# Hyena spectra: sums formed by VectorE from the accumulators, a smaller ScalarE copy, another order in the first unit, a buffer of its own for the last low products

## The chip, the cores and the metric

The program runs on one core of one Trainium2 chip. The metric is the device time of one execution in microseconds, median of several runs; lower is better. Engines are named as in the profile: PE (TensorE, matmuls), DVE (VectorE), ACT (ScalarE), POOL (GpSimd), SP (SyncE, which here only starts transfers).

## What is computed

Two transformer blocks on a sequence of 512 tokens of width 1024. The change touches only the Hyena mixer of the second block, whose core is a long convolution done through spectra, for two orders `o`:

```python
k2 = jnp.concatenate([fwd, jnp.zeros_like(fwd[:1]), bwd[1:][::-1]], axis=0)
k2 = k2 / jnp.sum(jnp.abs(k2), axis=0, keepdims=True)
kf = jnp.fft.rfft(k2, axis=0)
gates = (x1, x2)
zc = v
for o in range(HY_ORDER):
    zf = jnp.fft.rfft(zc.astype(jnp.float32), n=2 * L, axis=1)
    y = jnp.fft.irfft(zf * kf[None, :, o], n=2 * L, axis=1)[:, :L]
    zc = gates[o] * (y.astype(h.dtype) + skip[o] * zc)
return zc @ w_out
```

`fwd` and `bwd` are filters: the output of a small network, times a decay. L is 512.

## The kernel before

The whole program is one hand-ordered stream for each engine. Engines meet at semaphores alone: `then_inc(y_kc, 1)` raises one when an instruction ends, `wait_ge(y_kc, n)` holds the queue of an engine until it stands at n. Each queue runs strictly in order, so what is written first goes first.

The spectral stage works in four **units** u = 0 to 3: two orders times two halves of the 1024 channels. A unit's signal and filter are transformed with cosine and sine tables (`t_fwd`), in two halves f of the frequencies of 128 rows each, and back with `t_inv`. Since the spectrum of a real signal can be folded, the even and the odd time samples are transformed apart, and sums and differences of the two give the low and the high frequencies.

The steps of one unit, with their names in the code:

- `filter_tile(u, t, b)` (PE, L1684): two matmuls of the filter network's last layer into the accumulator banks b and b+1 of `ps`; `filter_out` (DVE, L2859, L2860) multiplies them with the decay DEC into PM, `y_pm`; `filter_abs` (ACT, L2228) writes their absolute values to the one buffer AB, `y_ab`, and waits for the sum before it, `y_n`; `filter_sum` (DVE, L2868 to L2872) adds them up in AS, `y_n`; `filter_norm` (PE) and `norm_out` (DVE) make the divisor.
- `turn_in(u)` (PE, L1728): transposes of the signal U into banks 4 and 5; `turned_in` (ACT, L2247) copies them to ZK, `y_tc`.
- `k_transform(u, f)` (PE, L1743): the filter's spectrum into banks 0 to 3 (cosine even, cosine odd, sine even, sine odd). `k_out` (ACT, L2253) copies all four to KS, `y_kc`. `k_parts` (POOL, L1129 to L1132) forms two sums and two differences of them in KP, `y_kp`. The next k_transform, and filter tiles that use these banks, wait for `y_kc`.
- `z_transform(u, f)` (PE, L1758): the signal's spectrum into banks 4 to 7; `z_even` (ACT, L2259) copies banks 4 and 6 to XZ.
- `multiply(u, f)` (DVE): the parts of z (L2899 to L2903, from XZ and banks 5 and 7, `y_x`), then the complex products in two halves (L2911 to L2917), each of six operations, into YB, `y_cb`.
- `y_parts(u, f)` (POOL, L1140 to L1144): sums and differences of YB into YF, `y_y`. For u > 0 it waits until `inverse(u - 1)` has read YF (`y_inv`).
- `inverse(u)` (PE, L1780): back to time; `gated` (DVE, L2934, L2936) scales, adds the skip term (`skipped`, ACT, L2267), and multiplies with the gate into U, `y_z`, from which the unit two later starts.

The four units overlap by hand: while DVE multiplies unit u, PE transforms the filter of u + 1 and the signal of u + 1, and the filter tiles of u + 2. In unit 0 the filter of unit 1 is also made inside this stage, in two pairs of tiles in banks 0 to 3, one pair ahead of z_transform(0,1) and one behind. In the last unit, the output projection (L536 to L538) follows directly on the last products.

KS has four rows of 512, and lies behind YF and ZK.

Of the kernel before, what the change touches and what calls it, by code (L numbers as in the profile page):

```python
# [122 lines left out]
def build(nc, A, out, stop=None):  # L123

    ctx = ExitStack()
    with ctx:
# [902 lines left out]
        def _(pool):  # L1029
# [93 lines left out]
            def k_parts(u, f):  # L1123

                pool.wait_ge(y_kc, 2 * u + f + 1)
                if u:
                    pool.wait_ge(y_cb, 4 * (u - 1) + 2 * f + 2)
                ce, co, se, so = (KS[:, n, :] for n in range(4))
                pool.tensor_tensor(KP[:, f, 0, :], ce, co, ALU.add)  # L1129
                pool.tensor_tensor(KP[:, f, 1, :], se, so, ALU.add)  # L1130
                pool.tensor_tensor(KP[:, f, 2, :], ce, co, ALU.subtract)
                pool.tensor_tensor(KP[:, f, 3, :], so, se, ALU.subtract).then_inc(y_kp, 1)  # L1132
# [1872 lines left out]
```

## Time and profile before

| | us |
|---|---|
| median of 3 runs | 2882.75 |
| lowest, highest | 2882.46, 2883.8 |
| the profiled execution: its time | 2882.58 |
| the profiled execution: its span | 2880.8 |
| PE busy in the span | 2777.3 (96%) |
| DVE, ACT, POOL busy | 1303.6 (45%), 712.7 (25%), 1606.7 (56%) |

The span is one execution from first to last instruction as the profiler recorded it; its time has a little around it. Busy time is the time in which an engine has an instruction in work. In the timelines below each row has a start in us from the span's start, a duration in us, the engine, the line of the code, the tiles written and read, and in brackets how long the engine idled before it and who released it. A row of PE with x16 is a merged run of 16 records; a float32 matmul leaves two. The granted clock (PEclk) of PE is 1.00 at 2.4 GHz and 0.50 at 1.2 GHz.

### The profile page before, as it was taken

The page shows a single profiled execution, that of the slowest core. Times are in us where ns is not written, and L with a number is a line of the kernel's source. Part 1 is how long each engine was busy: PE and PEld are TensorE (multiplying, and loading weights), DVE is VectorE, ACT ScalarE, POOL GpSimd, SP SyncE. Part 2 cuts the span into 40 slices and gives each one's busy share as a digit, 9 for nine tenths or more (in the row PEclk, how much of TensorE's full clock was granted, in tenths as well). Part 3 has the DMA queues.
Part 4 walks back from the last instruction along what each step waited for, and adds up shares of the span by engine and source line. Part 5 has one row for each costly group of instructions (what it writes and reads, how often), then busy time and mean ns, then how long its engine had stood idle before and what let it go on. Part 6 is the DMA issues. An engine that isn't in the chain of part 4 may idle for free.

```text
span 2880.8 us, 39841 instructions
## 1 busy us (share of the span) xinstructions
PE 2777.3 (96%) x15611; PEld 2250.4 (78%) x15611; DVE 1303.6 (45%) x1924; ACT 712.7 (25%) x1102; POOL 1606.7 (56%) x1569
## 2 busy tenths in 40 slices
PE   7999989999999999999999999999999898999999
PEld 7998888799678878888865568888777454788887
DVE  6787562211710564333346633331286678433311
ACT  3375224432620111110036621110111222211100
POOL 7652124655077766666641157766675534676764
PEclk9999999999999999999999999999999999999999
DMA  4221001222022564555530013332322100233331
GB/s 131 84 64 36 2 2 55 78 82 81 1 85 92 194 214 161 188 192 190 183 102 16 30 59 102 90 106 101 104 88 92 37 1 15 88 102 89 108 101 69
DMA packets 292585, 260.22 MB, mean 90 GB/s; under 512 B 6617, under 2 KB 264390, under 8 KB 292156
## 3 DMA queue, kind: packets, MB, share of 16 engines
q1 hardware_dynamic: 289492, 250.83, 27.1%
q0 software_dynamic: 2416, 6.34, 0.7%
q8 instruction: 117, 1.92, 0.3%
q10 hardware_dynamic: 504, 0.66, 0.1%
q14 instruction: 56, 0.46, 0.0%
HBM read 255.72 MB, written 2.10 MB: 89 GB/s over the span
## 4 chain that ended last, share of the span: by engine, by line
PE 87%; DVE 6%; issue 4%; DVEq 2%; ACT 2%; DMA 0%; POOL 0%; POOLq 0%; SPq 0%; ACTq 0%
PE ps L536 24%; PE ps L537 23%; PE ps L538 23%; PE ps L1780 2%; PE ps L1621 1%; PE ps L1758 1%; PE ps L1601 1%; PE ps L1611 1%; PE ps L1743 1%; PE ps L1366 1%; PE ps L1345 1%; PE ps L947 1%; DVE YB L2913 1%; PE ps L1373 1%; DVEq L2915 1%
## 5 line engine op out<-in xcount | busy, mean ns | idle before, releaser
L825 POOL CAST spl<-raw 128x512 fp32r<-128x512 f32 (+1 forms) x352 | 247.7, 704 | 635.0 <-PE ps L538 503.6
L536 PE MATMUL ps<-HSH,spl 128*128 128x512 f32 x1344 | 535.9, 399 | 20.4 <-DVE HSL L747 16.2
L827 POOL TENSOR_TENSOR spl<-raw,spl 128x512 fp32r<-128x512 f32 (+1 forms) x352 | 497.0, 1412 | 56.3 <-issue 6.5
L537 PE MATMUL ps<-HSL,spl 128*128 128x512 f32 x1344 | 527.3, 392 | 0.0
L538 PE MATMUL ps<-HSH,spl 128*128 128x512 f32 x1344 | 527.0, 392 | 0.0
L831 POOL TENSOR_TENSOR spl<-raw,spl 128x512 fp32r<-128x512 f32 (+1 forms) x352 | 481.2, 1367 | 51.5 <-issue 1.5
L536 PE MATMUL ps<-HNH,spl 128*128 128x264 f32 (+1 forms) x1152 | 364.7, 317 | 4.0 <-DVE HNL L717 3.6
L537 PE MATMUL ps<-HNL,spl 128*128 128x264 f32 (+1 forms) x1152 | 356.0, 309 | 0.0
L538 PE MATMUL ps<-HNH,spl 128*128 128x264 f32 (+1 forms) x1152 | 355.0, 308 | 0.0
L829 POOL CAST spl<-raw 128x512 fp32r<-128x512 f32 (+1 forms) x352 | 232.1, 659 | 206.8 <-PE ps L538 204.9
L536 PEld LDWEIGHTS ps<-HSH,spl 128*128 128x128 f32 x1344 | 254.2, 189 | 95.7 <-issue 38.5
L538 PEld LDWEIGHTS ps<-HSH,spl 128*128 128x128 f32 x1344 | 254.7, 190 | 54.3
L537 PEld LDWEIGHTS ps<-HSL,spl 128*128 128x128 f32 x1344 | 255.0, 190 | 52.6 <-issue 2.2
L536 PEld LDWEIGHTS ps<-HNH,spl 128*128 128x128 f32 x1152 | 217.5, 189 | 19.3 <-issue 5.2
L537 PEld LDWEIGHTS ps<-HNL,spl 128*128 128x128 f32 x1152 | 217.6, 189 | 13.3 <-issue 1.9
L538 PEld LDWEIGHTS ps<-HNH,spl 128*128 128x128 f32 x1152 | 216.9, 188 | 10.9
L536 PE MATMUL ps<-AFH,spl 128*128 128x512 f32 x528 | 206.2, 391 | 0.0
L538 PE MATMUL ps<-AFH,spl 128*128 128x512 f32 x528 | 205.6, 389 | 0.0
L537 PE MATMUL ps<-AFL,spl 128*128 128x512 f32 x528 | 205.5, 389 | 0.0
L2698 DVE TENSOR_TENSOR ps<-SG,ps 128x512 f32<-128x512 f32 x66 | 45.9, 696 | 259.7 <-PE ps L538 255.6
L2687 DVE SCALAR_TENSOR_TENSOR H<-ps,pcol,H 128x512 f32<-128x512 f32 x32 | 24.0, 751 | 276.5 <-PE ps L538 276.5
L937 DVE SCALAR_TENSOR_TENSOR ps<-adw,csil,ps 128x512 f32<-128x512 f32 x144 | 108.7, 755 | 46.5 <-DMA adw<-in_ada_w 36.0
(459 smaller groups left out, 4386.6 us busy)
## 6 DMA issues: line engine op xcount, KB each, us to landing
adw<-in_ada_w SPq DMA_DIRECT2D x96, 512.0 KB, 5.6
raw<-in_w_in SPq DMA_DIRECT2D x44, 1024.0 KB, 5.0
raw<-in_ffn_w_up SPq DMA_DIRECT2D x88, 512.0 KB, 4.6
raw<-in_w_ffn_in SPq DMA_DIRECT2D x44, 512.0 KB, 4.7
raw<-in_ffn_w_down SPq DMA_DIRECT2D x16, 1408.0 KB, 5.9
raw<-in_hy_w_in SPq DMA_DIRECT2D x12, 1024.0 KB, 5.0
raw<-in_w_ffn_out SPq DMA_DIRECT2D x8, 1408.0 KB, 6.4
raw<-in_w_branch_dn SPq DMA_DIRECT2D x8, 1024.0 KB, 4.9
```

The lines of the kernel that those rows point to most:

```text
L536: pe.matmul(dst, w[0], x[0], start=first, stop=False)
L537: pe.matmul(dst, w[0], x[1], start=False, stop=False)
L538: return pe.matmul(dst, w[1], x[0], start=False, stop=final)
L825: pool.tensor_copy(hi[:, first, :], w[:, first, :])
L827: pool.tensor_tensor(lo[:, first, :], w[:, first, :], hi[:, first, :], ALU.subtract).then_inc(split_first, 1)
L829: pool.tensor_copy(hi[:, second, :], w[:, second, :])
L831: pool.tensor_tensor(lo[:, second, :], w[:, second, :], hi[:, second, :], ALU.subtract).then_inc(split_ready, 1)
L937: ins = dve.scalar_tensor_tensor(ads[:, j % 2, :] if k == KD - 1 else acc, w, scale, acc, ALU.mult, ALU.add)
L947: mm = pe.matmul(ps[:, 4, ds(n, 1)], ads[:, j % 2, m * P:(m + 1) * P], ones[:, 0:1], start=True, stop=True)
L1345: mm = pe.matmul(ps[q, b, h * HALF:(h + 1) * HALF], G["lmp"][l % 2][q, h, :], G["yp"][q, h, :] if l else ident[q, q], start=True, stop=True)
L1780: mm = pe.matmul(dst, YF[:, f, e * 2 + s, c * P:(c + 1) * P], t_inv[:, s, f, e * SEQ // 2:(e + 1) * SEQ // 2], start=f + s == 0, stop=f + ...
L2698: dve.tensor_tensor(prod, SG[:, r % 2, :], ps[:, 2 * b, :], ALU.mult).then_inc(acc_free[b], 1)
```

## The change

- **k_parts moves from POOL to DVE.** ACT copies only banks 0 and 2 (the even parts) to KS, now of two rows; DVE adds and subtracts them with banks 1 and 3 read in place. Since banks 1 and 3 are now free only when DVE is done, PE's waits for `y_kc` become waits for `y_kp`, which DVE raises.
- **Unit 0 has another order.** z_transform(0,1) goes ahead of all filter tiles of unit 1; the four tiles follow in a row in banks 0, 2, 4 and 6. DVE does the parts of z of (0,1), the four filter products, and then the products of multiply(0,1) and the filter sums. turn_in(1) goes ahead of k_transform(1,1).
- **YL**, a buffer of four rows where KS was (and where KS now has two), takes the low products of the last unit, y_parts(3,0), which no longer waits for inverse(2).

```diff
@@
-        KS = fresh("KS", 4, SEQ)
+        ks_at = here[0]
+        KS = fresh("KS", 2, SEQ)
+        YL = at("YL", [4, SEQ], ks_at)
@@
+        def y_of(u, f, n):
+            return YL[:, n, :] if (u, f) == (UNITS - 1, 0) else YF[:, f, n, :]
@@ pool
             def y_parts(u, f):
-                if u:
+                if u and (u, f) != (UNITS - 1, 0):
                     pool.wait_ge(y_inv, u * NT)
...
-                if u + 1 < UNITS:
-                    k_parts(u + 1, 0)
                 y_parts(u, 1)
-                if u + 1 < UNITS:
-                    k_parts(u + 1, 1)
@@ tensor
             def k_transform(u, f):
                 if f:
-                    pe.wait_ge(y_kc, 2 * u + 1)
+                    pe.wait_ge(y_kp, 2 * u + 1)
...
             def filters(u):
                 filter_tile(u, 0, LATE_BANK[0])
-                pe.wait_ge(y_kc, 2 * u)
+                pe.wait_ge(y_kp, 2 * u)
...
             k_transform(0, 1)
-            pe.wait_ge(y_kc, 2)
-            filter_tile(1, 0, 0)
-            filter_tile(1, 1, 2)
             z_transform(0, 1)
-            pe.wait_ge(y_pm, NT + 1)
-            filter_tile(1, 2, 0)
-            pe.wait_ge(y_pm, NT + 2)
-            filter_tile(1, 3, 2)
+            pe.wait_ge(y_kp, 2)
+            for t in range(NT):
+                if t == 2:
+                    pe.wait_ge(y_x, 2)
+                filter_tile(1, t, FIRST_BANK[t])
@@ scalar
-                act.activation(KS[:, :, :], ps[:, 0:4, :], ACT.Copy).then_inc(y_kc, 1)
+                act.activation(KS[:, :, :], ps[:, 0:4:2, :], ACT.Copy).then_inc(y_kc, 1)
@@ vector
+            def k_parts(u, f):
+                dve.wait_ge(y_kc, 2 * u + f + 1)
+                dve.tensor_tensor(KP[:, f, 0, :], KS[:, 0, :], ps[:, 1, :], ALU.add)
+                dve.tensor_tensor(KP[:, f, 1, :], KS[:, 1, :], ps[:, 3, :], ALU.add)
+                dve.tensor_tensor(KP[:, f, 2, :], KS[:, 0, :], ps[:, 1, :], ALU.subtract)
+                dve.tensor_tensor(KP[:, f, 3, :], ps[:, 3, :], KS[:, 1, :], ALU.subtract).then_inc(y_kp, 1)
...
+            k_parts(0, 0)
             multiply(0, 0)
-            filter_out(1, 0, 0)
-            filter_out(1, 1, 2)
+            k_parts(0, 1)
+            parts_of_z(0, 1)
+            for t in range(NT):
+                filter_out(1, t, FIRST_BANK[t])
+            multiply(0, 1, parts=False)
             filter_sum(1, 0)
             filter_sum(1, 1)
-            filter_out(1, 2, 0)
-            filter_out(1, 3, 2)
-            multiply(0, 1)
+            k_parts(1, 0)
             filter_sum(1, 2)
             filter_sum(1, 3)
+            k_parts(1, 1)
...
             multiply(1, 0)
+            k_parts(2, 0)
             multiply(1, 1)
+            k_parts(2, 1)
...
             multiply(2, 0)
+            k_parts(3, 0)
             multiply(2, 1)
+            k_parts(3, 1)
             multiply(3, 0)
```

The first place is ACT in unit 0, from the transposes of unit 0 (ZK) to the skip terms of unit 0 (ytmp). Before:

```order
L2247 ACTIVATE ZK<-ps 128x512 [waits y_t] x4
L2253 ACTIVATE KS<-ps 128x2048 [waits y_k]
L2259 ACTIVATE XZ<-ps 128x1024 [waits y_dft]
L2253 ACTIVATE KS<-ps 128x2048 [waits y_kp,y_k]
L2228 ACTIVATE AB<-PM 128x1024 [waits y_n,y_pm] x2
L2259 ACTIVATE XZ<-ps 128x1024 [waits y_cb,y_dft]
L2228 ACTIVATE AB<-PM 128x1024 [waits y_n,y_pm]
L2253 ACTIVATE KS<-ps 128x2048 [waits y_kp,y_k]
L2228 ACTIVATE AB<-PM 128x1024 [waits y_n,y_pm]
L2247 ACTIVATE ZK<-ps 128x512 [waits y_t] x4
L2253 ACTIVATE KS<-ps 128x2048 [waits y_kp,y_k]
L2267 ACTIVATE ytmp<-U,pcol 128x512 [waits y_conv] x2
```

The same place with the change:

```order
L2238 ACTIVATE ZK<-ps 128x512 [waits y_t] x4
L2244 ACTIVATE KS<-ps 128x1024 [waits y_k]
L2250 ACTIVATE XZ<-ps 128x1024 [waits y_dft]
L2244 ACTIVATE KS<-ps 128x1024 [waits y_kp,y_k]
L2250 ACTIVATE XZ<-ps 128x1024 [waits y_cb,y_dft]
L2219 ACTIVATE AB<-PM 128x1024 [waits y_n,y_pm] x2
L2244 ACTIVATE KS<-ps 128x1024 [waits y_kp,y_k]
L2238 ACTIVATE ZK<-ps 128x512 [waits y_t] x4
L2219 ACTIVATE AB<-PM 128x1024 [waits y_n,y_pm] x2
L2244 ACTIVATE KS<-ps 128x1024 [waits y_kp,y_k]
L2258 ACTIVATE ytmp<-U,pcol 128x512 [waits y_conv] x2
```

The two AB copies of filter tiles (1,0) and (1,1) now stand behind the XZ copy of (0,1), and both ahead of the KS copy of k_transform(1,0) and the ZK copies of unit 1.

The second place is PE in unit 1, from the last transposes of turn_in(2) through the filter tiles of unit 3 to inverse(1); W_157 and A_158 are the weights and activations of the filter network. Before:

```order
L1728 MATMUL ps<-square,U 128x128 [waits y_tc]
L1728 MATMUL ps<-square,U 128x128 x3
L1684 MATMUL ps<-W_157,A_158 128x512 [waits y_w,y_am]
L1684 MATMUL ps<-W_157,A_158 128x512
L1684 MATMUL ps<-W_157,A_158 128x512 [waits y_kc]
L1684 MATMUL ps<-W_157,A_158 128x512 x3
L1684 MATMUL ps<-W_157,A_158 128x512 [waits y_tc]
L1684 MATMUL ps<-W_157,A_158 128x512
L1780 MATMUL ps<-t_inv,YF 128x256 [waits y_pm,y_y]
```

With the change:

```order
L1718 MATMUL ps<-square,U 128x128 [waits y_tc]
L1718 MATMUL ps<-square,U 128x128 x3
L1674 MATMUL ps<-W_157,A_158 128x512 [waits y_w,y_am]
L1674 MATMUL ps<-W_157,A_158 128x512
L1674 MATMUL ps<-W_157,A_158 128x512 [waits y_kp]
L1674 MATMUL ps<-W_157,A_158 128x512 x3
L1674 MATMUL ps<-W_157,A_158 128x512 [waits y_tc]
L1674 MATMUL ps<-W_157,A_158 128x512
L1770 MATMUL ps<-t_inv,YF 128x256 [waits y_pm,y_y]
```

The order is the same; the second tile's wait for ACT's copy has become a wait for DVE's sums.

The third place is DVE at the end of multiply(1,1). Before:

```order
L2916 TENSOR_TENSOR YB<-YB,YT 128x512
L2917 TENSOR_TENSOR YB<-YB,YT 128x512
L2859 TENSOR_TENSOR PM<-ps,DEC 128x512 [waits y_f,y_ab,y_w]
L2860 TENSOR_TENSOR PM<-ps,DEC 128x512
L2859 TENSOR_TENSOR PM<-ps,DEC 128x512 [waits y_f]
```

With the change:

```order
L2920 TENSOR_TENSOR YB<-YB,YT 128x512
L2921 TENSOR_TENSOR YB<-YB,YT 128x512
L2892 TENSOR_TENSOR KP<-KS,ps 128x512 [waits y_kc]
L2893 TENSOR_TENSOR KP<-KS,ps 128x512
L2894 TENSOR_TENSOR KP<-KS,ps 128x512
L2895 TENSOR_TENSOR KP<-ps,KS 128x512
L2853 TENSOR_TENSOR PM<-ps,DEC 128x512 [waits y_f,y_ab,y_w]
```

k_parts(2,1), four operations, stands between the last product and the filter products of unit 3.

## Rows read from the trace of the kernel before

**Rows 1.** The page of the profile: its head, and the chain's shares by engine.
```profile
span 2880.8 us, 39841 instructions
...
PE 87%; DVE 6%; issue 4%; DVEq 2%; ACT 2%; DMA 0%; POOL 0%; POOLq 0%; SPq 0%; ACTq 0%
```

**Rows 2.** Timeline of PE, 2225 to 2470: start, us, engine, line, [idle before <-releaser].
```profile
2260.13 3.60 PE L1684 MATMUL ps<-W,A 128*128 128x512 f32 x8
...
2266.13 8.76 PE L1743 MATMUL ps<-PM,t_fwd 128*128 128x512 f32 x16 [2.41 <-DVE PM L2860]
...
2276.85 7.13 PE L1743 MATMUL ps<-PM,t_fwd 128*128 128x512 f32 x16 [1.97 <-ACT KS L2253]
...
2294.99 13.98 PE L1780 MATMUL ps<-t_inv,YF 128*128 128x256 f32 x64
...
2350.51 15.74 PE L1780 MATMUL ps<-t_inv,YF 128*128 128x256 f32 x64 [2.91 <-DVE PM L2860]
...
2407.58 7.17 PE L1780 MATMUL ps<-t_inv,YF 128*128 128x256 f32 x32 [2.76 <-POOL YF L1144]
...
2433.67 6.90 PE L1780 MATMUL ps<-t_inv,YF 128*128 128x256 f32 x24 [5.15 <-POOL YF L1144]
...
2445.54 11.25 PE L1780 MATMUL ps<-t_inv,YF 128*128 128x256 f32 x40 [4.97 <-DVE U L2936]
...
2456.44 0.58 PE L536 MATMUL ps<-ZH,spl 128*128 128x512 f32 x1
```

**Rows 3.** Timeline of DVE, same columns, 2225 to 2447.
```profile
2242.04 0.69 DVE L2899 TENSOR_TENSOR XZ<-XZ,ps 128x512 f32<-128x512 f32 x1 [14.44 <-ACT XZ L2259]
...
2257.52 0.68 DVE L2860 TENSOR_TENSOR PM<-ps,DEC 128x512 f32<-128x512 f32 x1
...
2331.88 0.69 DVE L2899 TENSOR_TENSOR XZ<-XZ,ps 128x512 f32<-128x512 f32 x1 [1.22 <-ACT XZ L2259]
...
2334.69 1.55 DVE L2911 TENSOR_TENSOR YB<-XZ,KP 128x512 f32<-128x512 f32 x1 [0.16 <-issue]
...
2341.67 0.69 DVE L2911 TENSOR_TENSOR YB<-XZ,KP 128x512 f32<-128x512 f32 x1
...
2433.63 0.69 DVE L2911 TENSOR_TENSOR YB<-XZ,KP 128x512 f32<-128x512 f32 x1 [7.98 <-POOL YF L1144]
...
2437.59 0.69 DVE L2911 TENSOR_TENSOR YB<-XZ,KP 128x512 f32<-128x512 f32 x1
...
2443.76 0.75 DVE L2934 SCALAR_TENSOR_TENSOR ytmp<-ps,rn,ytmp 128x512 f32<-128x512 f32 x1 [0.16 <-issue]
```

**Rows 4.** Groups by line, 2225 to 2460: busy us, mean ns | idle before, releaser.
```profile
L2913 DVE TENSOR_TENSOR YB<-XZ,KP 128x512 f32<-128x512 f32 x16 | 20.6, 1284 | 0.0
...
L2899 DVE TENSOR_TENSOR XZ<-XZ,ps 128x512 f32<-128x512 f32 x8 | 5.5, 688 | 27.2 <-ACT XZ L2259 27.1
...
L2253 ACT ACTIVATE KS<-ps 128x2048 f32<-128x2048 f32 x8 | 15.0, 1876 | 32.8 <-PE ps L1743 32.8
...
L2259 ACT ACTIVATE XZ<-ps 128x1024 f32<-128x1024 f32 x8 | 8.2, 1021 | 49.7 <-PE ps L1758 33.6 <-DVE YB L2917 16.2
...
L2228 ACT ACTIVATE AB<-PM 128x1024 f32<-128x1024 f32 x12 | 12.7, 1056 | 26.8 <-DVE PM L2860 16.4 <-DVE AS L2872 8.7 <-DVE AS L2868 1.7
...
L1129 POOL TENSOR_TENSOR KP<-KS 128x512 f32<-128x512 f32 x8 | 10.9, 1359 | 36.4 <-ACT KS L2253 36.4
```

**Rows 5.** Timeline of POOL, 2215 to 2470.
```profile
2256.14 1.72 POOL L1140 TENSOR_TENSOR YF<-YB 128x512 f32<-128x512 f32 x1
...
2428.61 1.26 POOL L1140 TENSOR_TENSOR YF<-YB 128x512 f32<-128x512 f32 x1 [15.28 <-PE ps L1780]
```

**Rows 6.** Busy time of stretches: length, each engine's busy us, PEclk, DMA share, GB/s.
```profile
2266.00:2269.50 3.50, 3.37 (x4) 1.51 (x5) 3.17 (x6) 0.00 (x0) 1.83 (x3) 0.51 0.42 95
...
2408.00:2411.50 3.50, 3.50 (x18) 3.09 (x17) 3.34 (x4) 0.00 (x0) 3.50 (x3) 1.00 0.00 0
...
2446.00:2449.50 3.50, 3.50 (x9) 2.56 (x9) 3.42 (x5) 2.01 (x4) 2.61 (x3) 0.50 0.02 5
```

More of the change, by code:

```diff
@@ L1121, in filter_in @@
                 pool.dma_start(DEC[:, :, :], dec[:, :, half_d]).then_inc(y_w, 16)
-            def k_parts(u, f):
-                pool.wait_ge(y_kc, 2 * u + f + 1)
-                if u:
[L1127 to L1132, printed above, removed]
             def y_parts(u, f):
-                if u:
+                if u and (u, f) != (UNITS - 1, 0):
                     pool.wait_ge(y_inv, u * NT)
                 c, si, cm, sm = (YB[:, n, :] for n in range(4))
+                y = [y_of(u, f, n) for n in range(4)]
                 pool.wait_ge(y_cb, 4 * u + 2 * f + 1)
-                pool.tensor_tensor(YF[:, f, 0, :], c, cm, ALU.add)
-                pool.tensor_tensor(YF[:, f, 2, :], c, cm, ALU.subtract)
+                pool.tensor_tensor(y[0], c, cm, ALU.add)
+                pool.tensor_tensor(y[2], c, cm, ALU.subtract)
                 pool.wait_ge(y_cb, 4 * u + 2 * f + 2)
-                pool.tensor_tensor(YF[:, f, 1, :], si, sm, ALU.subtract)
-                pool.tensor_tensor(YF[:, f, 3, :], si, sm, ALU.add).then_inc(y_y, 1)
+                pool.tensor_tensor(y[1], si, sm, ALU.subtract)
+                pool.tensor_tensor(y[3], si, sm, ALU.add).then_inc(y_y, 1)
             pool_split(pool, hy_in, behind_second=mlp_in)
@@ L1789, in inverse @@
                 else:
-                    pe.wait_ge(y_kc, 2 * UNITS)
+                    pe.wait_ge(y_kp, 2 * UNITS)
                 for c in cs:
@@ L1795, in inverse @@
                         for f in range(2):
-                            mm = y_products(ps[:, c % 2 if u + 2 < UNITS else c, e * SEQ // 2:(e + 1) * SEQ // 2], c, e, f)
+                            mm = y_products(u, ps[:, c % 2 if u + 2 < UNITS else c, e * SEQ // 2:(e + 1) * SEQ // 2], c, e, f)
                     mm.then_inc(y_inv, 1)
@@ L1821, in _ @@
                     z_transform(u, 1)
+                else:
+                    turn_in(u + 1)
                 k_transform(u + 1, 1)
-                turn_in(u + 1)
+                if u:
+                    turn_in(u + 1)
                 if u + 2 < UNITS:
@@ L2277, in _ @@
             k_out(0, 1)
+            z_even(0, 1)
             filter_abs(1, 0)
-            filter_abs(1, 1)
-            z_even(0, 1)
-            filter_abs(1, 2)
             for u in range(UNITS):
@@ L2284, in _ @@
                     z_even(u, 0)
+                if u == 0:
+                    filter_abs(1, 1)
                 if u + 1 < UNITS:
                     k_out(u + 1, 0)
+                if 0 < u < UNITS - 1:
+                    z_even(u, 1)
                 if u == 0:
+                    turned_in(1)
+                    filter_abs(1, 2)
                     filter_abs(1, 3)
+                    k_out(1, 1)
                 elif u + 1 < UNITS:
-                    z_even(u, 1)
-                if u + 1 < UNITS:
                     turned_in(u + 1)
@@ L2894, in _, with parts_of_z @@
                         norm_out(0, 6)
-            def multiply(u, f):
+            def k_parts(u, f):
[4 more added lines that the diff above has]
+                dve.tensor_tensor(KP[:, f, 3, :], ps[:, 3, :], KS[:, 1, :], ALU.subtract).then_inc(y_kp, 1)
+            def parts_of_z(u, f):
                 dve.wait_ge(y_zc, 2 * u + f + 1)
@@ L2903, in multiply @@
                 dve.tensor_tensor(XZ[:, 1, :], XZ[:, 1, :], ps[:, 7, :], ALU.add).then_inc(y_x, 1)
+            def multiply(u, f, parts=True):
+                if parts:
+                    parts_of_z(u, f)
                 dve.drain()
-                dve.wait_ge(y_kp, 2 * u + f + 1)
                 if u or f:
```

15 lines of the change are left out of this document (7 added, 8 removed).

## The prediction

> **What bounds the kernel now.** The page of the profile comes first: of a span of 2880.8 us, PE carries 87% of the chain that ended last and DVE 6% [rows 1]. The diff touches one stage only, the spectral part of the Hyena mixer, from the last projection tile to the first matmul of the output projection at 2456.44. So the timelines of that stage are read next, and in them PE's brackets: how long PE idled and for whom. Rows 2 hold the places. PE waits 2.41 us for the filter product PM ahead of k_transform(1,0), 1.97 us for the copy KS, 2.91 us for PM ahead of inverse(1), 2.76 us for YF ahead of inverse(2), and 5.15 and 4.97 us in the last unit [rows 2]. Between these waits PE's work is the same before and after; the change moves only the waits. Behind every one of them stands a chain on DVE, so DVE's timeline [rows 3] gives the prices, and the groups by line [rows 4] the means.
>
> **Prices.** A multiply() is three pieces on DVE. The even and odd parts of z take 2.74 us in unit 0 (2242.04 to the first product, 0.69 us an operation) and 2.81 us at 2331.88 [rows 3]. A half of the products takes 3.96 us where POOL is quiet (2433.63 to 2437.59) and 6.17 us where POOL forms YF beside it (2437.59 to 2443.76); where POOL still forms KP, as at 2334.69 to 2341.67, it takes 6.98 us [rows 3]. The reason is visible in one operation: L2913, with both inputs in SBUF, has a mean of 1284 ns, against 688 ns for L2899, which has one input in ps [rows 4]. L2860 with an input in ps took 0.68 us at 2257.52 [rows 3], while POOL's L1140 was running from 2256.14 [rows 5]. So I cost the new k_parts on DVE, four operations of L2899's form, at about 0.61 us start to start, 2.5 us in all with the semaphore wait, and do not stretch it beside POOL. Its bounds are 2.4 us (four at the pace of rows 3) and 4.7 us (two of the four held up by POOL as a half of products is, (6.17 - 3.96) / 2 = 1.1 us each).
> The Trainium skill speaks against this price (VectorE: DVE Perf Modes, section "The TRN2 errata"): its table gives VectorE 120 fixed cycles from PSUM and 58 from SBUF at 0.96 GHz. Here the two are 688 ns and 0.69 us, so the trace does not agree; by the page five k_parts on the path would add about 5 x 4 x 65 ns = 1.3 us, an estimate.
> On ACT, KS shrinks from four banks, 1876 ns, to two, which I take at the 1021 ns of XZ, an activation of 1024 elements [rows 4]. POOL loses eight times four operations with a mean near 1359 ns [rows 4]; this is worth time only where POOL was late or in DVE's way. A pair of filter tiles takes 3.60 us, so 1.72 us a tile, start to start; a transform takes 7.1 us for 16 records [rows 2].
>
> **Unit 0: a loss.** Until 2242.04 nothing moves: k_parts(0,0) ends near 2237.7, hidden behind z_transform(0,0). multiply(0,0) then takes 2.7 + 4.0 + 6.2 us and ends near 2254.9, k_parts(0,1) near 2257.4, and PE, which has finished z_transform(0,1) at 2254.5, waits 3.0 us for it. Four tiles and the last filter_out follow; k_transform(1,0) starts near 2266.0, where it starts now (2266.13 [rows 2]). But DVE now has the products of multiply(0,1) behind the filter products, 4.0 + 6.2 us, to 2276.1. Only then comes filter_sum(1,0), and this matters, since the new ACT order puts filter_abs(1,1) ahead of k_out(1,0): the single buffer AB must be read first. Queued on ACT behind it are KS and all four ZK copies. So: first sum 0.7 us (2276.8), AB 1.06 us (2277.9), KS 1.0 us (2278.9); meanwhile filter_sum(1,1) to 2280.4; k_parts(1,0) 2.5 us, and k_transform(1,1) starts at 2282.9 instead of 2276.85, 6.1 us later. Behind it, 18.1 us now pass until inverse(0) at 2294.99 [rows 2]; then it will be 6.9 for the transform, 1.2 for the copy, 2.6 for k_parts, 0.9 for the norm and 5.2 for three tiles, 16.8 us, since the turn_in lies in the hole: -1.3 us. The clock: k_transform(1,0) took 8.76 us where the later one took 7.13 [rows 2], with a granted clock of 0.51 in its first 3.5 us [rows 6], so a restart after such a wait costs 1.7 us. It is now hidden for k_transform(1,0) and comes back at k_transform(1,1), ahead of which PE idles 5.4 and 2.5 us with 1 us of transposes between: +1.7. Unit 0 gives **+6.5 us**.
>
> **Unit 1: a loss.** multiply(1,0) is unchanged. k_parts(2,0), 2.5 us, takes the place of DVE's 1.22 us wait for XZ [rows 3], which it covers: +1.3. The first half of multiply(1,1) no longer has POOL beside it: 6.98 - 3.96 = -3.0. DVE is then 1.7 us earlier. But k_parts(2,1), 2.5 us, follows, and filter tile (3,1) now waits for it (y_kp) where it waited for ACT's copy (y_kc), done long before. Three tiles, 5.2 us, which now hide behind DVE, stand in the open: -1.7 + 2.5 + 5.2, and 0.1 for the signal, is 6.1 us against the 2.7 us by which inverse(1) now follows the last product. **+3.4 us**. The wait of 2.91 us and its clock loss [rows 2] move from inverse(1) to the tiles.
>
> **Unit 2: even.** The same trade (+1.3, -3.0, +2.5) brings k_parts(3,1) to the moment at which YF is ready. k_transform(3,1) waits 3.0 us for k_parts(3,0), and z_transform(3,0) ends just where the 2.76 us wait [rows 2] ends now. **+0.1 us**.
>
> **Unit 3: the gain.** z_transform(3,0) ends later, so DVE starts multiply(3,0) 2.85 us later; its first half loses POOL's company, -3.0; its second half gains it, +2.2, since y_parts(3,0) writes YL and no longer waits for inverse(2) (POOL waited 15.28 us for it [rows 5]); the two gated() take 0.9 us more beside POOL. Together +2.9. In return DVE's wait of 7.98 us for YF [rows 3] goes. The products of multiply(3,1), and with them the 4.97 us wait of PE and the output projection, come 8.0 - 2.9 = 5.1 us earlier against inverse(2). What is late next is the same DVE chain, now without a hole. **-5.1 us**.
>
> **Sum.** 6.5 + 3.4 + 0.1 - 5.1 = +4.9 us, with three clock losses as now. Two restarts are new, both after 3.0 us of idle: the tiles behind k_parts(0,1), and k_transform(3,1). Of the five waits over 2.3 us in rows 2, four are followed by slow records; the one of 2.76 us is not (7.17 us for 32, granted clock 1.00 [rows 6]). Two times 1.7 us at four in five is +2.7. Total **+7.6 us**. The profiled run took 2882.58 us with its span of 2880.8, 0.2 us under the median of 2882.75, so the forecast is 2882.58 + 7.6 = **2890.2 us**.
>
> **Rivals.**
> - *The clock forgives* (the other side, not slower). If neither new restart falls to 0.5, the sum is +4.9, 2887.5; if the hole in unit 0 costs nothing either, about +3, 2885.5. A measurement of this kernel can tell about 0.2%, 5.8 us, so this is no change. It decides at the two waits of 3.0 us: with one of them charged the sum is 6.6. For it speaks the 2.76 us wait, against it the 2.41 us one, which was charged. 0.32.
> - *The clock takes more.* PE's two short bursts of work between long waits at the end now had 0.50 still 4 us after the restart [rows 6] and lost 2.5 us (11.25 for 40 records). If the hole of unit 0 does that, and both restarts are charged: +10 to +12, 2893 to 2895. I count it with the forecast: 0.60 for both.
> - *POOL and k_parts collide.* Then five k_parts grow by up to 2.2 us: up to +11 on the forecast, 2896 to 2901. Rows 3 and 5 show the form untouched. 0.03.
> - *Faster.* This needs DVE's order in unit 0 not to bite: were filter_sum(1,0) done before 2270, unit 0 would lose nothing and the total would be -1 to +1, still no change; over 5.8 us faster also needs all restarts free and a second gain of 5 us. The wait of filter_abs(1,1) on the sum is in the code. 0.05, with all else I have not seen.
>
> **Numbers.** Slower by over 0.2%: 0.60 + 0.03 = 0.63; within 0.2%: 0.32; faster: 0.05. The range takes in both clock cases: 2884.0 to 2895.5.
>
> **What would show it.** PE idle for DVE's k_parts near 2254 to 2257; an ACT wait of some 14 us at the second AB behind a DVE sum; k_transform(1,1) at 2283; tile (3,1) released by k_parts(2,1); no wait of DVE for YL or YF in unit 3; the granted clock at 0.5 in the four restarts. If k_parts takes more than 2.7 us, if half a multiply beside nothing is not 4.0 us, or if k_transform(1,1) starts before 2278, the prediction is wrong in that step.

## The result, and the profile after

| | before | changed |
|---|---|---|
| median of 13 runs, us | 2882.75 (2881.11 to 2886.26) | 2890.75 (2887.72 to 2893.5) |
| profiled run, us; its span, us | 2882.58; 2880.8 | 2890.96; 2889.2 |
| mean granted clock in the profiled run | 0.985 | 0.982 |

The ratio is 1.0024, with a 95% interval from 1.0017 to 1.0031: the changed kernel is slower by 8.0 us, where 7.6 had been forecast. The head of the page and the chain by engine answer to [rows 1]:

```profile
span 2889.2 us, 39827 instructions
...
PE 2782.8 (96%) x15611; PEld 2252.9 (78%) x15611; DVE 1316.7 (46%) x1956; ACT 706.6 (24%) x1102; POOL 1564.2 (54%) x1537
...
PE 87%; DVE 6%; issue 4%; DVEq 2%; ACT 1%; DMA 0%; POOL 0%; POOLq 0%; SPq 0%; ACTq 0%
```

POOL has lost 42.5 us of work (it had 1606.7) and DVE has gained 13.1 (it had 1303.6), and the chain is the same, PE and then DVE. The totals say nothing of where the 8 us are. The timeline of PE does; it answers to [rows 2], with the same columns:

```profile
2225.90 1.11 PE L1718 MATMUL ps<-square,U 128*128 128x128 f32 x8
...
2258.80 7.14 PE L1674 MATMUL ps<-W,A 128*128 128x512 f32 x16 [2.80 <-DVE KP L2895]
2267.32 7.13 PE L1733 MATMUL ps<-PM,t_fwd 128*128 128x512 f32 x16 [1.38 <-DVE PM L2854]
2274.30 1.11 PE L1718 MATMUL ps<-square,U 128*128 128x128 f32 x8
2281.86 1.98 PE L1718 MATMUL ps<-square,U 128*128 128x128 f32 x8 [6.45 <-ACT ZK L2238]
2284.90 8.60 PE L1733 MATMUL ps<-PM,t_fwd 128*128 128x512 f32 x16 [1.05 <-DVE KP L2895]
...
2297.13 1.05 PE L1681 MATMUL ps<-ones,AS 128*128 128x1 f32 x8 [1.91 <-DVE KP L2895]
2298.04 7.09 PE L1674 MATMUL ps<-W,A 128*128 128x512 f32 x12
2304.97 13.98 PE L1770 MATMUL ps<-t_inv,YF 128*128 128x256 f32 x64
...
2343.21 10.16 PE L1733 MATMUL ps<-PM,t_fwd 128*128 128x512 f32 x16 [2.76 <-DVE KP L2895]
...
2359.87 6.94 PE L1674 MATMUL ps<-W,A 128*128 128x512 f32 x12 [2.40 <-DVE KP L2895]
2366.65 13.98 PE L1770 MATMUL ps<-t_inv,YF 128*128 128x256 f32 x64
...
2404.88 7.13 PE L1733 MATMUL ps<-PM,t_fwd 128*128 128x512 f32 x16 [2.76 <-DVE KP L2895]
...
2422.06 7.07 PE L1770 MATMUL ps<-t_inv,YF 128*128 128x256 f32 x32
...
2454.45 3.78 PE L1770 MATMUL ps<-t_inv,YL 128*128 128x256 f32 x8 [6.36 <-DVE U L2940]
2458.02 7.34 PE L1770 MATMUL ps<-t_inv,YF 128*128 128x256 f32 x32
2465.01 0.58 PE L539 MATMUL ps<-ZH,spl 128*128 128x512 f32 x1
```

The start of each inverse() cuts the stage into four pieces, unit 0 from turn_in(0) to inverse(0), and so on; unit 3 ends with the first matmul of the output projection. The table gives their lengths in us, for both kernels and for six others of the next section, each from its own timeline of PE. The last column but one is the time that PE's records lost to the clock. It is worked out from the records: sixteen of 128x512 take 7.03 us at the full clock, twelve 5.4, eight 3.6, sixty-four of 128x256 13.98, forty 8.8, thirty-two 7.07, twenty-four 5.34, eight about 1.8, and what a row takes beyond that is counted. Not counted are excesses of about 0.1 us and the transposes of 128x128 (0.9 us behind the long wait for ZK in e2 and in the changed kernel, where PE waits again behind them). The column is good to some 0.1 us, and it is the sum over all rows, on the critical path or off it.

| kernel | unit 0 | unit 1 | unit 2 | unit 3 | stage | clock loss | ratio to before (95%) |
|---|---|---|---|---|---|---|---|
| before | 70.48 | 55.52 | 57.07 | 48.86 | 231.93 | 7.5 | |
| before, second profile (e11) | 71.22 | 55.50 | 57.08 | 49.04 | 232.84 | 9.7 | |
| changed | 79.07 | 61.68 | 55.41 | 42.95 | 239.11 | 10.2 | 1.0024 (1.0017 to 1.0031) |
| YL alone (e1) | 70.49 | 55.52 | 57.08 | 42.86 | 225.95 | 5.2 | 0.9979 (0.9970 to 0.9988) |
| YL and the new order, sums on POOL (e2) | 72.04 | 55.52 | 58.37 | 43.12 | 229.05 | 6.7 | 0.9986 (0.9977 to 0.9995) |
| e2 with the first sum ahead (e7) | 67.69 | 55.50 | 57.07 | 44.18 | 224.44 | 6.7 | 0.9976 (0.9966 to 0.9987) |
| YL and sums on DVE, old order (e3) | 89.29 | 60.58 | 57.11 | 42.73 | 249.71 | 12.7 | 1.0061 (1.0047 to 1.0075) |
| changed, with the first sum ahead (e4) | 75.08 | 58.88 | 55.41 | 42.91 | 232.28 | 7.4 | 1.0000 (0.9991 to 1.0009) |
| e1 with PE kept busy at two waits (e8) | 71.52 | 56.48 | 55.31 | 42.76 | 226.07 | 3.4 | 0.9977 (0.9968 to 0.9986) |

The ratios go by runs of the kernel before that were made beside each kernel, with medians of 2882.5 to 2884.0 us, so they differ by up to 0.0006 from quotients with 2882.75.

Between the kernel before and the changed one, units 0 and 1 lose 8.6 and 6.2 us, and units 2 and 3 gain 1.7 and 5.9: +7.2 us in all. The profiled runs differ by 8.4. The other 1.2 us lie outside the stage, which starts at 2225.90 where it started at 2224.51 (1.4 us later, of which 0.2 come back behind it). That is no work of the change: the two profiles of one and the same kernel before start it at 2224.51 and 2225.27, and in the twelve profiles of this study it starts anywhere between 2222.58 and 2226.73. So the stage's length is the better measure, and it is used below.

Four rows explain most of the changed kernel. They stand in the timelines of ACT, of DVE, and of DVE again, in units 0, 1 and 3:

```profile
2279.35 1.06 ACT L2219 ACTIVATE AB<-PM 128x1024 f32<-128x1024 f32 x1 [15.57 <-DVE AS L2862]
```
```profile
2277.53 1.73 DVE L2862 TENSOR_TENSOR AS<-AB 128x512 f32<-128x512 f32 x1 [0.16 <-issue]
...
2357.34 0.69 DVE L2892 TENSOR_TENSOR KP<-KS,ps 128x512 f32<-128x512 f32 x1 [1.39 <-ACT KS L2244]
...
2442.54 0.69 DVE L2915 TENSOR_TENSOR YB<-XZ,KP 128x512 f32<-128x512 f32 x1
```

ACT stands 15.57 us at the second AB copy, because the sum that frees AB runs at 2277.53 on DVE, behind the products of multiply(0,1). k_parts(2,1) finds KS late by 1.39 us. And the first product of multiply(3,1), which waited 7.98 us for YF in [rows 3], waits for nothing.

### The profile page after: what moved, and what is told of

Read it like the earlier page. It is cut to its first block, busy times and chain, and to the rows that moved or that the text cites. A ratio compares the mean times of both kernels' runs of the same rounds, so it can differ in the third digit from the quotient of the medians.

```text
span 2889.2 us, 39827 instructions
## 1 busy us (share of the span) xinstructions
PE 2782.8 (96%) x15611; PEld 2252.9 (78%) x15611; DVE 1316.7 (46%) x1956; ACT 706.6 (24%) x1102; POOL 1564.2 (54%) x1537
## 4 chain that ended last, share of the span: by engine, by line
PE 87%; DVE 6%; issue 4%; DVEq 2%; ACT 1%; DMA 0%; POOL 0%; POOLq 0%; SPq 0%; ACTq 0%
PE ps L539 24%; PE ps L540 23%; PE ps L541 23%; PE ps L1770 1%; PE ps L1733 1%; PE ps L1611 1%; PE ps L1748 1%; PE ps L1674 1%; PE ps L1591 1%; PE ps L1601 1%; PE ps L1356 1%; PE ps L1335 1%; PE ps L953 1%; PE ps L1363 1%; PE ps L1267 1%
```

## The experiments

**Each half of the change alone.** Four kernels take the change apart: YL, the order of unit 0, and the place of the sums. e1 is the kernel before with only this:

```diff
+        ks_at = here[0]
         KS = fresh("KS", 4, SEQ)
+        YL = at("YL", [4, SEQ], ks_at)
...
-                if u:
+                if u and (u, f) != (UNITS - 1, 0):
                     pool.wait_ge(y_inv, u * NT)
+                if (u, f) == (UNITS - 1, 0):
+                    pool.wait_ge(y_kp, 2 * UNITS)
```

> Kernel before plus one part of the change alone: the low products of the last unit go to a buffer of their own (YL, laid over KS, which has been read by then), so y_parts(3,0) no longer waits for inverse(2). KP stays on POOL, the orders stay. Theory (the step on unit 3 of the prediction, and the gain of 5.9 us seen there in the changed kernel): DVE's wait of 7.98 us for YF goes, the products of multiply(3,1) and the output projection come 4.8 to 5.9 us earlier; 2877 to 2878 us, against 2882.75. Rival: the gain of the last stretch belongs to POOL freed from KP, and with KP still there y_parts(3,0) comes no earlier than multiply(3,1) needs it, or the ten final us lose it again in a deeper clock loss: under 2 us gained, 2881 to 2883 us.

Measured: 2877.14 us, ratio 0.9979, 6 us faster; all of it lies in unit 3, 42.86 us against 48.86. Two timelines of e1, of POOL and of PE:

```profile
2414.08 1.76 POOL L1148 TENSOR_TENSOR YL<-YB 128x512 f32<-128x512 f32 x1 [2.66 <-DVE YB L2925]
```
```profile
2438.44 3.54 PE L1788 MATMUL ps<-t_inv,YL 128*128 128x256 f32 x8 [6.57 <-DVE U L2944]
2441.82 7.07 PE L1788 MATMUL ps<-t_inv,YF 128*128 128x256 f32 x32
2448.53 0.58 PE L538 MATMUL ps<-ZH,spl 128*128 128x512 f32 x1
```

POOL's first operation on YL follows DVE's YB after 2.66 us, not inverse(2), for which the same operation waited 15.28 us in [rows 5]. The theory holds, and the rival falls: the gain needs no freed POOL.

e2 is the changed kernel with k_parts back on POOL and a KS of four banks, and with the order of unit 0 and YL as changed:

```diff
-        KS = fresh("KS", 2, SEQ)
+        KS = fresh("KS", 4, SEQ)
...
+            k_parts(0, 0)
+            k_parts(0, 1)
             y_parts(0, 0)
...
-                act.activation(KS[:, :, :], ps[:, 0:4:2, :], ACT.Copy).then_inc(y_kc, 1)
+                act.activation(KS[:, :, :], ps[:, 0:4, :], ACT.Copy).then_inc(y_kc, 1)
...
-            k_parts(0, 0)
             multiply(0, 0)
-            k_parts(0, 1)
```

> The changed kernel with one part undone: the four sums KP are again formed on POOL from a four-bank copy on ACT; the new order of unit 0 and YL stay. Theory (the sums on DVE are what costs): order and YL together stand 3.2 us under the kernel before, by adding up the durations of the rows, and the new place of the sums costs 7 to 10 us; 2879 to 2881 us. Rival (the new order of unit 0 is what costs, since the products of multiply(0,1) stand ahead of filter_sum(1,0)): the loss of 6 to 8.6 us in unit 0 stays and only units 1 and 2 recover 4 us; 2886 to 2888 us.

Measured: 2880.38 us, ratio 0.9986. The stage takes 229.05 us, 2.9 under before (3.2 had been worked out) and 10.1 under the changed kernel. So the sums on DVE cost 10 us in the new order, up to 3.5 of them by a larger clock loss, and without them the new order costs 1.6 us in unit 0. The rival, the order as the whole cause, falls: it left 6 to 8.6 us in unit 0. But the sum that frees AB is late here too, as ACT's timeline of e2 shows, and e4 and e7 below price that:

```profile
2274.78 1.06 ACT L2237 ACTIVATE AB<-PM 128x1024 f32<-128x1024 f32 x1 [11.73 <-DVE AS L2880]
```

e3 is the other half undone, the order of unit 0 as before on PE, ACT and DVE, with the sums on DVE:

```diff
-            z_transform(0, 1)
             pe.wait_ge(y_kp, 2)
-            for t in range(NT):
-                if t == 2:
-                    pe.wait_ge(y_x, 2)
-                filter_tile(1, t, FIRST_BANK[t])
+            filter_tile(1, 0, 0)
+            filter_tile(1, 1, 2)
+            z_transform(0, 1)
+            pe.wait_ge(y_pm, NT + 1)
+            filter_tile(1, 2, 0)
+            pe.wait_ge(y_pm, NT + 2)
+            filter_tile(1, 3, 2)
```

> The changed kernel with the other part undone: unit 0 runs in the order of the kernel before on PE, ACT and DVE; the sums stay on DVE and YL stays. Theory (the sums cost, the order repays part of it): with two filter sums, two filter copies and then both k_parts ahead of it on DVE the first product of multiply(0,1) comes later still; adding up the rows puts the output projection 12 us behind the kernel before with the old order and YL, 8 us behind the changed kernel; 2895 to 2899 us. Rival (the order is what costs): the 8.6 us that the changed kernel loses in unit 0 come back but for the 2.5 us of one k_parts on the path; 2884 to 2886 us.

Measured: 2901.06 us, ratio 1.0061; the stage takes 249.71 us, 10.6 more than in the changed kernel. The theory had 8, and its 2895 to 2899 us were missed by 2; the clock column accounts for the rest, 12.7 us lost here against 10.2. The rival, 2884 to 2886 us, falls by 15 us. Its timeline of PE shows why the order was changed at all:

```profile
2255.83 6.33 PE L1674 MATMUL ps<-W,A 128*128 128x512 f32 x8 [9.66 <-DVE KP L2891]
...
2289.62 9.94 PE L1733 MATMUL ps<-PM,t_fwd 128*128 128x512 f32 x16 [8.64 <-DVE KP L2891]
```

PE's first filter tile needs banks that only k_parts(0,1) frees, and k_parts(0,1) is queued on DVE behind all of multiply(0,0): 9.66 us of waiting, and 8.64 us at the next such place. The four kernels make a square. The new order costs 3.1 us of stage with the sums on POOL (229.05 - 225.95) and saves 10.6 with the sums on DVE (249.71 - 239.11). The sums on DVE cost 23.8 us in the old order and 10.1 in the new. Neither edit has a price of its own. These four differences hold the clock with the work: by the clock column up to 1.5, 2.5, 7.5 and 3.5 us of them, in the order named.

**The queue on DVE in unit 0.** e4 is the changed kernel with one filter sum ahead of the products, and k_parts(1,0) ahead of the second:

```diff
+            filter_sum(1, 0)
             multiply(0, 1, parts=False)
-            filter_sum(1, 0)
-            filter_sum(1, 1)
             k_parts(1, 0)
+            filter_sum(1, 1)
             filter_sum(1, 2)
```

> The changed kernel with DVE's order changed in two places of unit 0: filter_sum(1,0) stands ahead of the products of multiply(0,1), and k_parts(1,0) ahead of filter_sum(1,1). Theory (unit 0 loses because AB, and behind it KS and ZK on ACT, wait for a sum that is queued behind ten us of products): ACT's wait of 15.6 us at the second AB shrinks to about 5, k_transform(1,1) is released some 4 us earlier, the products end 0.7 us later; 3.7 us under the changed kernel, 2887.0 us, within 1.5. Rival (PE in unit 0 is held by the products and the clock, not by the sum): within 1 us of the changed kernel, 2890 to 2892 us.

Measured: 2883.77 us, ratio 1.0000, 7 us under the changed kernel, where 3.7 were expected. The timelines of ACT and PE:

```profile
2266.37 1.06 ACT L2219 ACTIVATE AB<-PM 128x1024 f32<-128x1024 f32 x1 [4.18 <-DVE AS L2862]
```
```profile
2279.07 8.83 PE L1733 MATMUL ps<-PM,t_fwd 128*128 128x512 f32 x16 [3.36 <-DVE KP L2895]
```

ACT waits 4.18 us instead of 15.57, and k_transform(1,1) starts 54.77 us after the start of the stage instead of 59.00: unit 0 is 4.0 us shorter, as the theory has it. The other 2.8 us are in unit 1, where nothing was changed: k_transform(2,1) loses 1.7 us to the clock instead of 3.1, and the tiles behind it, which lost 1.5, lose nothing.

e7 makes the same edit with the sums on POOL:

```diff
+            filter_sum(1, 0)
             multiply(0, 1, parts=False)
-            filter_sum(1, 0)
             filter_sum(1, 1)
```

> The sums on POOL, YL, the new order of unit 0, and filter_sum(1,0) ahead of the products of multiply(0,1): everything of the change but the sums on DVE, with the order mended. Theory: unit 0 took 72.0 us with the sums on POOL and the new order; its k_transform(1,1) waited for ACT's copies, which waited for the sum; the sum ahead takes 2 to 3 us off, so unit 0 takes 69 to 70 us, about one less than the order of before, and the whole stage 224.5 to 227: 2876 to 2878 us, level with the kernel that has YL alone. Rival (with KP on POOL, k_transform(1,1) and the products are bound by KP, not by the sum): unit 0 stays at 72 us, 2880 us.

Measured: 2876.08 us, ratio 0.9976. Unit 0 takes 67.69 us, 4.35 less than in e2 and 2.8 less than before; 2 to 3 had been expected. Part of the 4.35 is clock: k_transform(1,1) lost 1.7 us in e2, and nothing here, where PE waits 1.51 us for ZK instead of 4.16. It is the fastest kernel of the study by its median, but its interval and that of YL alone overlap nearly whole, so that the reordering has gained nothing that the times can tell. In the stage it is 1.5 us ahead of YL alone, after a clock loss that is 1.5 us larger.

**The price of one k_parts.** e6b is the changed kernel with the four sums of k_parts(2,1) formed twice, and a drain between:

```diff
             def k_parts(u, f, again=False):
                 dve.wait_ge(y_kc, 2 * u + f + 1)
+                if again:
+                    dve.tensor_tensor(KP[:, f, 0, :], KS[:, 0, :], ps[:, 1, :], ALU.add)
...
+                    dve.drain()
```

> The changed kernel with the four sums of k_parts(2,1) formed twice on DVE (the same values, a drain of DVE between the two sets). It measures the price of one k_parts and whether that of (2,1) lies on the path to inverse(1), as the step on unit 1 of the prediction has it. Theory: four more operations at 0.60 us start to start and 0.1 to 0.2 us for the drain; the tiles (3,1) to (3,3) and inverse(1) start 2.5 us later and nothing takes it back, so the interval from inverse(0) to inverse(1) goes from 61.7 to 64.2 us, plus or minus one clock loss. Rival 1 (the sums are hidden behind PE's tiles or YF): under 1 us. Rival 2 (an operation with an input in ps costs more once four more stand in a row, or POOL stretches it): 3.3 to 4.7 us.

Measured: 2895.41 us, ratio 1.0044 (1.0029 to 1.0058); unit 1 takes 64.73 us against 61.68. The timelines of DVE and PE there:

```profile
2358.31 0.69 DVE L2893 TENSOR_TENSOR KP<-KS,ps 128x512 f32<-128x512 f32 x1 [1.43 <-ACT KS L2244]
...
2360.87 0.69 DVE L2898 TENSOR_TENSOR KP<-KS,ps 128x512 f32<-128x512 f32 x1
...
2363.27 0.68 DVE L2853 TENSOR_TENSOR PM<-ps,DEC 128x512 f32<-128x512 f32 x1
```
```profile
2363.41 7.39 PE L1674 MATMUL ps<-W,A 128*128 128x512 f32 x12 [4.96 <-DVE KP L2901]
```

The extra set takes 2.56 us (2358.31 to 2360.87), 4 x 0.60 and 0.16 for the drain, and PE's wait grows from 2.40 to 4.96 us, by the same 2.56. Nothing hides it: k_parts(2,1) lies on the path to inverse(1), whole. The other 0.5 us are clock (7.39 for the twelve records instead of 6.94). By the medians the kernel lost 4.7 us, more than this 3.05: k_transform(3,1), the one restart of unit 2, lost 1.5 us here and nothing in the changed kernel. The Trainium skill (VectorE: DVE Perf Modes, section "The TRN2 errata") gives VectorE 120 fixed cycles from PSUM and 58 from SBUF; by that each of these operations would carry 62 more, an estimate. The trace does not show it: 0.60 us start to start for the sums that read ps, 0.60 to 0.61 for the products that read SBUF alone.

**The clock.** Two kernels and two repeats ask what takes PE's clock. e5 is the changed kernel with PE kept busy in its longest hole:

```diff
                 for t in range(NT):
+                    if t == 2 and u == 1:
+                        for _ in range(7):
+                            pe.matmul(ps[:, 6, :], t_fwd[:, 0, 0, 0:P], PM[:, 0, 0, :], start=True, stop=True)
                     if t >= 2:
```

> The changed kernel plus seven matmuls of 128x512 whose result is thrown away, on PE in the hole of unit 0 (inside turn_in(1), ahead of the wait for the second ZK copies); the granted clock is the only thing they can change for the better. Theory (1.6 us of k_transform(1,1) and 1.5 us of the tiles behind it are a clock loss after the 6.45 us wait): with PE busy for about 3 us of that wait, k_transform(1,1) takes 7.1 us and the tiles 5.4; 1.5 to 3.2 us under the changed kernel, 2887.5 to 2889.3 us. Rival (the slow records have another cause, or the clock falls at the waits of 1.05 and 1.91 us that stay): no change in these records, 2890 to 2892 us.

Measured: 2889.74 us, ratio 1.0022 (1.0013 to 1.0031), the same as the changed kernel. The timeline of PE:

```profile
2275.20 6.17 PE L1717 MATMUL ps<-PM,t_fwd 128*128 128x512 f32 x14
2281.82 1.23 PE L1721 MATMUL ps<-square,U 128*128 128x128 f32 x8 [0.44 <-ACT ZK L2241]
2284.85 8.62 PE L1736 MATMUL ps<-PM,t_fwd 128*128 128x512 f32 x16 [1.80 <-DVE KP L2898]
```

Of 7.5 us of idle time ahead of k_transform(1,1), 0.44 and 1.80 are left (each matmul shows as two records, and the seven took 6.2 us, not 3), and it takes 8.62 us as before (8.60). The time lies between the two ranges, so the records decide, and the tiles behind it took 7.10 us as before (7.09): the theory falls. The hole of 6.45 us is not what the loss hangs on. Here the slow records follow a wait of 1.80 us.

e8 does it on the kernel with YL alone, at the waits of 2.42 and 2.91 us for PM:

```diff
+            def busy(b, pm, n):
+                pe.wait_ge(y_pm, pm)
+                for _ in range(n):
+                    pe.matmul(ps[:, b, 0:SEQ // 2], t_fwd[:, 0, 0, 0:P], t_fwd[:, 0, 0, :], start=True, stop=True)
...
             def k_transform(u, f):
+                if (u, f) == (1, 0):
+                    busy(1, 2 * NT - 1, 5)
...
             def inverse(u, cs=range(NT)):
+                if u == 1:
+                    busy(6, 3 * NT + 1, 5)
```

> The kernel before with YL, plus five matmuls of 128x256 whose result is thrown away at each of two waits of PE for PM: ahead of k_transform(1,0) and ahead of inverse(1), placed behind the filter product before the last one, whose bank they use. PE's idle time of 2.42 and 2.91 us is cut into about 1.2 to 1.6 us and a rest. Theory (the clock falls for the idle time ahead of a record): k_transform(1,0) takes 7.1 instead of 8.76 us and inverse(1) 14.0 instead of 15.74; 3.3 us under the kernel with YL alone, 2873 to 2874.5 us. Rival (cutting the wait is not enough, the clock still falls, and the extra matmuls stand in the way): both records as slow as now, 2877 to 2878 us.

Measured: 2877.37 us, ratio 0.9977, level with e1 (2877.14). The timeline of PE in unit 0:

```profile
2265.84 2.43 PE L1742 MATMUL ps<-t_fwd 128*128 128x256 f32 x10 [1.23 <-DVE PM L2877]
2268.10 7.03 PE L1758 MATMUL ps<-PM,t_fwd 128*128 128x512 f32 x16
2277.10 8.83 PE L1758 MATMUL ps<-PM,t_fwd 128*128 128x512 f32 x16 [1.97 <-ACT KS L2270]
```

Both records named run at the full clock now (7.03, and 13.98 for inverse(1)), so that half of the theory holds, and the gain is not there for two reasons. The five matmuls took 2.43 us where 1.2 us of the wait was left, so each place starts about 1 us later. And k_transform(1,1), which lost nothing after 1.97 us in e1, loses 1.8 after the same 1.97 us here: the loss has moved to the next wait. That the added matmuls moved it is not shown by this one profile, since in e11 below the same transform loses 1.8 us with nothing added.

e10 and e11 are the two kernels once more, unaltered, for a second profile.

> The changed kernel once more, unaltered, for a second profile: which of PE's restarts lose clock. In the first profile k_transform(1,1) lost 1.6 us, the tiles behind it 1.7, k_transform(2,1) 3.0, the tiles (3,1) to (3,3) 1.6, the last products 2.0, and the restarts after 2.80 us (unit 0) and 2.76 us (unit 2) nothing. Theory A (what a restart loses hangs on the lengths of the waits and what stands before them): the same records lose the same again, since every wait is the same to 0.1 us. Theory B (it hangs on when the restart falls, which differs from execution to execution): the waits are the same again but at least two of the seven restarts change between charged and not charged, or by over 1 us, and the span moves by as much.

> The kernel before once more, unaltered, for a second profile of its restarts. In the first one k_transform(1,0) lost 1.7 us after 2.41 us of waiting, inverse(1) 1.75 after 2.91, the last unit 1.6 and 2.5, and inverse(2) nothing after 2.76. Theory A (the loss hangs on the waits): the same again. Theory B (it hangs on when the restart falls in the execution): the same waits, another set of losses, among them a loss at inverse(2) or none at k_transform(1,0) or inverse(1).

Measured: 2890.37 and 2884.29 us, one run each. In the changed kernel the second profile repeats the first in every record, each within 0.05 us, and the stage within 0.1 (239.18): theory A. In the kernel before it does not. Its timeline of PE in unit 0, second profile:

```profile
2250.47 5.41 PE L1684 MATMUL ps<-W,A 128*128 128x512 f32 x8 [1.97 <-ACT KS L2253]
...
2267.56 7.13 PE L1743 MATMUL ps<-PM,t_fwd 128*128 128x512 f32 x16 [1.38 <-DVE PM L2860]
2276.66 8.83 PE L1743 MATMUL ps<-PM,t_fwd 128*128 128x512 f32 x16 [1.97 <-ACT KS L2253]
```

The first of these rows in the first profile of the kernel before, and in e8:

```profile
2249.72 3.71 PE L1684 MATMUL ps<-W,A 128*128 128x512 f32 x8 [1.97 <-ACT KS L2253]
```
```profile
2250.60 3.71 PE L1692 MATMUL ps<-W,A 128*128 128x512 f32 x8 [1.97 <-ACT KS L2270]
```

The tiles after the first KS wait lose 1.8 us and took 3.71 in the first profile; k_transform(1,0) loses nothing and lost 1.7 in [rows 2], and because the tiles are later its wait is 1.38 us and not 2.41; k_transform(1,1) loses 1.8 and lost nothing. Theory B holds here, in unit 0, and A in the other units (each record within 0.2 us). So the wait alone does not decide. Nor does the time since the start of the span: in e8, whose order up to there is the same, these tiles start 0.13 us later than in e11, after the same 1.97 us, and lose nothing. And in the four profiles with the changed kernel's unit 0 (changed, e10, e5, e6b) the stage starts between 2225.26 and 2226.73, while k_transform(1,1), the tiles behind it and k_transform(2,1) lose the same in all four, to 0.1 us. What else decides is left open: no experiment moved a restart in time with all else the same.

## Why the prediction was right, and where it was so by chance

**Unit 0, +6.5 forecast, +8.6 measured.** Every step is in the trace. k_transform(1,0) starts 41.42 us after the start of the stage, and 41.62 before: unmoved. The second AB copy waits 15.57 us (some 14 forecast), and k_transform(1,1) starts 6.66 us later (6.1). Between them the size of one row was wrong: the first filter sum takes 1.73 us and not 0.7. It reads both inputs from SBUF, and POOL forms YF beside it from 2277.45 on; in e4 and e7, where POOL forms nothing beside it, it takes 0.68. What follows takes 20.07 us; without its clock losses 16.8, the figure of the prediction. The loss at k_transform(1,1) came as forecast, 1.57 for 1.7. But the tiles behind k_parts(1,1), ahead of which PE waits 1.91 us, lost 1.7 more, a restart that the sum did not have. The sum's place in DVE's queue is half of the loss: it is worth 4.0 us in e4, and 4.35 in e7 with the sums on POOL (1.7 of them clock). The other half is the sums: e4 and e7 have the same order up to k_parts(1,0) and take 75.08 and 67.69 us in unit 0, with 3.5 us and none lost to the clock, so 3.9 us are work that k_parts adds on DVE. (Against the kernel before, e4 is 4.6 us longer in unit 0: these 3.9, and 1.8 more of clock, less 1.1 that the order with the sum ahead saves.)

**Unit 1, +3.4 forecast, +6.2 measured.** The mechanism held: k_parts(2,1) stands ahead of the tiles, nothing covers it (e6b), and three tiles stand in the open. From the last product to inverse(1) it takes 10.7 us (2355.94 to 2366.65), where 2.5 + 5.2 + 0.1 = 7.8 had been summed. The 2.9 us between are both the clock's: k_transform(2,1) lost 3.1 us, so KS came 1.39 us late for DVE, and the tiles lost 1.5, which is the loss that the prediction had moved there without a term in this sum. In e4, where k_transform(2,1) lost 1.7 and the tiles nothing, the same unit takes 58.88 us, 3.4 more than before: the forecast to a tenth.

**Unit 2, +0.1 forecast, -1.7 measured.** The work did not change, as forecast; the 1.75 us that inverse(1) loses in [rows 2] fell into this interval before, and into unit 1 (1.5 us, at the tiles) now. The prediction had said so of the loss but did not book it to a unit.

**Unit 3, -5.1 forecast, -5.9 measured.** DVE's first product of multiply(3,1) comes 20.5 us after inverse(2) instead of 26.1, 5.6 us earlier. The last records lose 2.2 us to the clock instead of 2.5. e1 gives the same 6.0 us by itself, so the term is the buffer's alone.

**The clock, +2.7 forecast.** The total is right and both of its places are wrong. Busy time of five stretches in the changed kernel, columns as in [rows 6]:

```profile
2258.80:2262.30 3.50, 3.50 (x8) 1.69 (x9) 3.38 (x6) 0.00 (x0) 0.00 (x0) 1.00 0.00 0
...
2298.00:2301.50 3.50, 3.50 (x6) 1.47 (x6) 0.40 (x2) 1.06 (x1) 0.00 (x0) 0.52 0.00 0
2343.20:2346.70 3.50, 3.49 (x4) 1.51 (x5) 3.29 (x6) 0.00 (x0) 0.00 (x0) 0.50 0.00 0
...
2359.90:2363.40 3.50, 3.50 (x5) 1.67 (x6) 1.11 (x2) 1.06 (x1) 0.00 (x0) 0.56 0.00 0
2404.90:2408.40 3.50, 3.50 (x8) 1.61 (x9) 3.31 (x6) 0.00 (x0) 0.00 (x0) 1.00 0.00 0
```

The two new restarts that were priced at 1.7 us each at four in five ran at a granted clock of 1.00, 2.4 GHz, after 2.80 and 2.76 us of idle. The three losses that were to stay or move did so: 1.6 us at k_transform(1,1), 1.5 at the tiles (3,1) to (3,3) after 2.40 us, 2.2 at the end. Two restarts stood nowhere in the sum, and both were charged: the tiles after 1.91 us lost 1.7, and k_transform(2,1), after 2.76 us, lost 3.1. That second wait was overlooked. PE waits for k_parts(2,0) ahead of k_transform(2,1) just as it does for k_parts(3,0) ahead of k_transform(3,1), and the prediction names only the latter. Before, k_transform(2,1) started with no wait, as PE's timeline of the kernel before has it:

```profile
2330.29 7.03 PE L1743 MATMUL ps<-PM,t_fwd 128*128 128x512 f32 x16
```

Over all rows the loss rose from 7.5 to 10.2 us, which is the 2.7 forecast only by chance: 1.6 us of the old loss, at the 24 records of [rows 2] ahead of the wait of 4.97 us, are gone, and they never lay on the path; and of the 3.1 us at k_transform(2,1) only 1.4 reached DVE, as its wait for KS.

Two steps failed here. One left out the wait ahead of k_transform(2,1) and the one of 1.91 us. The other read "of the five waits over 2.3 us, four are followed by slow records" as a rule on the length of the wait; the prediction's own rival, the row of 2.41 us against the one of 2.76, had the evidence against it.

So the work's terms are right by their steps, and the last microsecond is luck. The medians differ by 8.0 us, with an interval of about 4.9 to 8.9: the forecast of 7.6 lies 0.4 us under the 8.0, but of the 8.4 us between the profiled runs 1.2 are the drift of the start of the stage, which was in no term, and the stage itself gave 7.2.

**What would have beaten both.** The change as a whole was three edits, of which one was worth 6 us, one cost 10 and one was there to keep that cost from being 24. The buffer alone is 0.21% faster than the kernel before, and with the order changed and the first sum ahead 0.24%.

## What to carry to other kernels

A reordering that comes with a move of work to another engine is priced with it and not apart: find on the receiving engine what stands ahead of the moved work, and who waits for what stands behind it. A single buffer that is freed by a short operation (AB, 15.57 us of ACT's time for one sum) wants that operation ahead of any long batch, and moving it there gave 7 us back, 4 of its own and 3 of the clock. Look for every wait that the move makes, also where PE ran through before. Where PE waits some 2 us at several places, put the clock's loss down as a range for the whole stage, not as a price for each wait.
